# Multiplications by the identity at six places where TensorE waits

## The reference

```python
# first block: mixed attention, then a mixture of 16384 tiny experts (PEER)
s1, s2 = scores of the two query halves against 128 + 128 keys, 8 heads
eidx, gate = the 16 best pairs per head and token, softmax of their scores
act = gelu(x . expert_u[eidx])            # "scores" in the kernel
y   = sum(gate * act * expert_v[eidx])    # "values" in the kernel
# second block
x = x + parallel_mixer(rms_norm(x))                # convolution and a linear recurrence
x = x + cross_attention(rms_norm(x), rms_norm(mem))
x = x + moe(rms_norm(x))                           # 4 groups of 4 experts:
#   best group, its two best experts, out = sum_e combine[e] * (silu(t Wg) * (t Wu)) Wd
out = rms_norm(x)
```

## Time and profile before

| | us |
|---|---|
| Executions shown | 1901.77, 1902.85, 1911.56 |
| Median | 1902.85 |
| Profiled execution, its own time | 1907.88 |
| Its span, first to last instruction | 1906.2 |

### The profile page before, as it was taken

How to read it: one execution, slowest core, us unless ns; L and a number is a source line. 1 busy time by engine, 2 the same in 40 slices (tenths; PEclk the granted TensorE clock), 3 DMA queues, 4 the chain that set the end, 5 groups by cost and what they waited for, 6 DMA issues and landing times.

```text
span 1906.2 us, 25804 instructions
## 1 busy us (share of the span) xinstructions
PE 1840.6 (97%) x10066; PEld 1574.2 (83%) x10066; DVE 1316.9 (69%) x1857; ACT 911.5 (48%) x1013; POOL 77.6 (4%) x101
## 2 busy tenths in 40 slices
PE   8999998999999999999999999989989899999997
PEld 4778766888898888999999999888979778888885
DVE  5788687668998664555555555567865678888887
ACT  2544463412234344444444444455644467667665
POOL 0000000100000341110000000000000000000000
PEclk9999898999999999999999999999999899999999
DMA  7655354434446795666555555554333579898894
GB/s 307 244 190 193 120 206 159 177 111 144 170 150 221 234 284 197 220 203 217 179 195 179 195 178 196 179 199 158 134 140 117 213 304 347 316 354 333 327 351 155
DMA packets 61697, 404.94 MB, mean 212 GB/s; under 512 B 8129, under 2 KB 8417, under 8 KB 15281
## 3 DMA queue, kind: packets, MB, share of 16 engines
q1 hardware_dynamic: 51904, 371.22, 53.2%
q0 software_dynamic: 5968, 20.82, 3.8%
q10 hardware_dynamic: 3746, 11.83, 1.9%
HBM read 391.25 MB, written 12.58 MB: 212 GB/s over the span
## 4 chain that ended last, share of the span: by engine, by line
PE 87%; DVE 6%; DMA 3%; ACT 2%; issue 1%; DVEq 0%; ACTq 0%; SPq 0%
PE ps L2322 23%; PE ps L2323 23%; PE ps L2324 23%; PE ps L2428 7%; PE ps L2725 3%; DMA raw<-in_stream_dram 1%; DMA BIG<-in_stream_dram 1%; PE ps L2901 1%; ACT whi L692 1%; DVE wlo L1239 1%; PE ps L2438 1%; PE ps L2784 1%; PE ps L2559 1%; PE ps L2538 1%; DVE H L1273 0%
## 5 line engine op out<-in xcount | busy, mean ns | idle before, releaser
L1239 DVE TENSOR_TENSOR wlo<-raw,whi 128x2048 fp32r<-128x2048 f32 x179 | 410.1, 2292 | 325.2 <-ACT whi L692 325.1
L692 ACT ACTIVATE whi<-raw 128x2048 fp32r<-128x2048 f32 x179 | 342.9, 1916 | 398.1 <-PE ps L2324 384.6
L2322 PE MATMUL ps<-thi,whi 128*128 128x256 f32 x1056 | 300.7, 285 | 2.1 <-DVE tlo L1256 2.0
L2323 PE MATMUL ps<-tlo,whi 128*128 128x256 f32 x1056 | 300.0, 284 | 0.0
L2324 PE MATMUL ps<-thi,wlo 128*128 128x256 f32 x1056 | 299.9, 284 | 0.0
L2322 PE MATMUL ps<-whi,phi 128*128 128x512 f32 x608 | 239.6, 394 | 7.5 <-DVE plo L1830 6.1
L2322 PE MATMUL ps<-whi,thi 128*128 128x512 f32 (+1 forms) x576 | 228.7, 397 | 10.8 <-DVE wlo L1239 10.7
L2323 PE MATMUL ps<-wlo,phi 128*128 128x512 f32 x608 | 238.5, 392 | 0.0
L2324 PE MATMUL ps<-whi,plo 128*128 128x512 f32 x608 | 237.8, 391 | 0.0
L2324 PE MATMUL ps<-whi,tlo 128*128 128x512 f32 (+1 forms) x576 | 225.1, 391 | 0.0
L2323 PE MATMUL ps<-wlo,thi 128*128 128x512 f32 (+1 forms) x576 | 224.5, 390 | 0.0
(11 more groups left out here) (411 smaller groups left out, 2659.4 us busy)
## 6 DMA issues: line engine op xcount, KB each, us to landing
raw<-in_stream_dram SPq DMA_DIRECT2D x259, 1024.0 KB, 4.8
BIG<-in_stream_dram SPq DMA_DIRECT2D x84, 1024.0 KB, 6.9
BIG<-g_spill POOLq DMA_DIRECT2D x64, 128.0 KB, 4.8
BIG<-in_stream_dram SPq DMA_DIRECT2D x2, 2048.0 KB, 16.4
spare<-in_stream_dram SPq DMA_DIRECT2D x4, 1024.0 KB, 6.1
g_spill<-H ACTq DMA_DIRECT2D x4, 1024.0 KB, 4.8
g_spill<-MOD ACTq DMA_DIRECT2D x4, 1024.0 KB, 4.8
MID<-in_gains_dram POOLq DMA_DIRECT2D x7, 512.0 KB, 4.0
```

Source lines behind the costliest of these rows:

```text
L692: nc.scalar.activation(whi[:, u % 2, :], raw_of(u), ACT.Copy).then_inc(unit_hi, 1)
L1239: nc.vector.tensor_tensor(wlo[:, u % 2, :], raw_of(u), whi[:, u % 2, :].bitcast(f32), ALU.subtract).then_inc(unit_split, 1)
L2322: nc.tensor.matmul(out, ahi, bhi, start=start, stop=False)
L2323: nc.tensor.matmul(out, ahi, blo, start=False, stop=False)
```

## The change

A helper multiplies `ident` by `iota` into 256 columns of a bank that nobody reads at that time, and six calls of it stand ahead of waits. Nobody reads what it writes, and it sets no semaphore.

```diff
+            def run_on(bank, times):
+
+                for _ in range(times):
+                    nc.tensor.matmul(ps[:, bank, 0:S], ident[:, :], iota[:, :], start=True, stop=True)
+
...
+            run_on(2, 9)
             pe.wait_ge(gelu_done, EARLY)
             pe.wait_ge(g_free, 2 * S // GT)
...
+            run_on(7, 8)
             transposes(T_MIX, H)
...
+            run_on(7, 3)
             transposes(T_HX, H)
...
+            run_on(7, 3)
             for k in range(4):
                 t = k // 2
                 pe.wait_ge(rows_ready, ROWS[T_HF] - 2 * TT + k + 1)
...
+            run_on(7, 5)
             pe.wait_ge(grp_ready, 1)
             counts = ps[:, 7, 0:(TT + 1) * N_GRP]
...
+            run_on(6, 3)
             gather(0)
```

## The result

| | executions | median us | range us | ratio to before (95%) |
|---|---|---|---|---|
| Changed kernel, first | 5 | 1891.53 | 1888.16 to 1900.28 | 0.9948 (0.9926 to 0.9970) |
| The same, again | 12 | 1896.09 | 1891.36 to 1906.85 | 0.9974 (0.9957 to 0.9991) |
| The same, a third time | 12 | 1897.48 | 1891.52 to 1903.31 | 0.9971 (0.9958 to 0.9985) |
| Before, beside the last two | 52 | 1902.32 | 1896.79 to 1911.41 | |

The change makes the kernel faster. The first measurement says 11.3 us between the medians (ratio 0.9948), with 1891.53 outside the forecast's range; the 24 later executions of the same kernel have a median of 1896.68, so 5.6 us (0.3%).

The account below looks back on a forecast made before the run. PE's time was taken as the kernel's outside a few waits, at full or half clock. Terms 2.90 + 0 + 2.1 + 2.9 = 7.9 us off 1907.88 give 1900.0; 60% off the median gives 1898.2; between them 1899, range 1893 to 1905.

Parts of the forecast that it names:

- The range: Whole kernel: 1893 (clock held throughout) to 1905 (only the first values gain), about 1 in 10 beyond on either side.
- The gain goes through: First values: full clock from the first product saves 2.90 us, since PE hardly waits from there to 1239 us; bounds 0 and 2.90.
- the prediction's own condition for failure: Fails if the clock falls ahead of the values, or a wait for DVE or a load takes the gain back before 1490.
- The 60%: Whole kernel: from the median only 60% of the 7.9 us gain, 4.7, is taken, giving 1898.2.
- Mixer's norm: Mixer norm's transposes: gain 0, because DVE's low parts fix the first product; bounds -1.7 and +0.2 us.
- the case of the lower bound, -1.7: Mixer's norm: PE idles again behind the transposes and the clock may fall where the products start, half of 3.4 us.
- Cross-attention's norm: Products behind the cross-attention norm: 4.49 us at half clock, of which 2.1 is saved; bounds 0 and 2.1.
- Routing: Router, group counts and gather: 2.9 us saved, between 1.8 (clock fallen in mid-router) and 5.3 (held throughout); bounds -2.9 and 5.3.
- transposes don't hold the clock: Rival, 0.11: at three transpose stages idle time counts on through the transposes; only the values' 2.90 stays, 1905.0.
- Identity times a ramp does not count: Rival, 0.08: added multiplications don't count as work, the clock falls as before, routing runs overrun by 2.9 us: 1910.8 or 1905.8.
- Done already: Rival, 0.13: the profile caught the worst instants; the median execution gains only the first values' part, cut down: about 1902.
- The clock holds through the router as well: Rival, 0.10: routing saves 5.3 us in place of 2.9: 1897.6 from the profile, about 1893 on a good execution.

Follow-up runs that it names:

- with transposes: Changed kernel with each added multiplication replaced by four 128x128 transposes of the identity: 1893.97 us, ratio 0.9951 to the kernel before.
- routing alone: Of the six added runs only the three at the routing (router's transposes, group counts, gather) are kept: 1902.49 us, ratio 0.9998 to the kernel before.
- the last two experiments: Changed kernel with G loads cut to an eighth in the first 18 units, with and without the run of nine: values stage 620.90 and 623.84 us.
- without values: Changed kernel without the run of nine multiplications ahead of the first values, the other five runs standing: 1893.67 us, ratio 0.9956 to the kernel before.
- without the five: Changed kernel without the run of five multiplications ahead of the group counts, the other five runs standing: 1895.54 us, ratio 0.9966 to the kernel before.
- norms alone: Of the six added runs only those ahead of the mixer's and cross-attention norm's transposes are kept: 1899.50 us, ratio 0.9986 to the kernel before.
- values alone: Of the six added runs only the run of nine ahead of the first values is kept: 1902.30 us, ratio 0.9999 to the kernel before.
- twelve-run kernel: Eleven-run kernel plus a run of 3 multiplications ahead of the first attention transposes: 1888.67 us, ratio 0.9925 to the kernel before.
- eleven-run kernel: Changed kernel with five more added runs at idle places followed by half clock: 1887.90 us, ratio 0.9918 to the kernel before.

## Why the prediction was wrong

The direction, the mechanism and most of the places were right; the size was not: 1891.53 first, 1896.7 later, where 1899 was said. Three steps failed, and a loss that the prediction named but counted at nothing, at the mixer's norm, came true in part.

**The range.** "The range goes from 1893 to 1905" was built from the mechanism's cases only. Executions of one kernel spread over 15 us, and the first five had a median 5 us below that of the next 24, of which two are as low as 1891.53 and 21 lie in the forecast's range. A term for where five executions' median falls was missing. Why those five were low isn't settled: three had a clock of 0.990 to 0.993, so less half clock than most; whether by chance or by the chip used, no run tells.

**"The gain goes through"** at the first values. The clock part came as forecast (full clock from 619.17, pace 0.23), and the prediction's own condition for failure, a load that takes it back, came true. In the changed kernel, in order of time:

```profile
703.84 1.92 ACT L692 ACTIVATE whi<-raw 128x2048 fp32r<-128x2048 f32 x1 [4.92 <-DMA raw<-in_stream_dram]
...
708.83 0.47 PE L2322 MATMUL ps<-whi,phi 128*128 128x512 f32 x1 [1.54 <-DVE plo L1830]
```

The 1 MB load for this unit was issued at 695.31 and landed at 703.81, 8.5 us, while a unit's 24 products need 5.4. Before, the load at that point took 6.8 (698.17 to 705.01), and PE didn't wait. PE waited 0.73 to 1.54 us there in seven of the eight profiles with a run ahead of the values and whole loads; the eighth, with transposes, had a load of 6.8 us, no wait, and the shortest stage of them, 621.69. One of the four without a run (routing alone) waited 1.18. The earlier trace rows showed that PE hardly waited, but not how little the loads had to spare; the last two experiments show, in one execution each, that with small G loads the wait is gone and the gain stands. The term was 2.90 and measures 0.7 to 1.1.

**The 60%.** "From the median I therefore take only 60%" rested on the thought that an execution with later falls has part of the gain already. The two sets of executions (24 and 52) say otherwise: the changed kernel is 5.2 us lower at the tenth part of its executions from below (1893.66 against 1898.86), 5.6 at the median, 5.2 at the tenth part from above (1901.07 against 1906.29). Good and bad executions gain alike, since falls vary also where nothing was changed (the column "ahead"). The step's 4.7 us came near the 5.6 only because the sum that it cut, 7.9, was more than 2 too large; and the mean of it with 1900.0, the sum taken off a slow execution, left 3.85.

The other terms, from the stages of the table:
- *Mixer's norm*, forecast 0: 8.16 to 8.21 us with the run, 8.28 to 8.38 without, 0.15. DVE's low parts set the first product, as said. But the case of the lower bound, -1.7 ("the clock may now fall where the products start"), came true in four of eleven profiles with the run, where the fall in the transposes had cost nothing. Three of them are in the table (third, without values, without the five), and their mixer stage took 181.74 to 181.83 us, against 180.35 before and 180.24 with the norms alone. In the first two profiles of the changed kernel it took 181.44 and 181.02 for another reason: the low stretch at 1320 to 1326 lasted 6.8 us in place of 3.4.
- *Cross-attention's norm*, forecast 2.1: 66.56 to 66.59 in four profiles of the table, 68.06 and 68.07 in two where the clock fell 0.4 us after the first product in spite of the run; 68.35 to 68.55 without. 2.0 or 0.4, in the mean 1.4.
- *Routing*, forecast 2.9 between 1.8 and 5.3. Two cases occur: held through the router or most of it, with late counts (router 3.72 to 4.01 us, DVE's wait 1.01 to 1.31, stage 19.93 to 19.95), and fallen in the router (21.55, 21.56). Held throughout, with the counts on time, is in no profile with the runs. Against the mean 23.7 of the three without runs (23.99, 25.46, 21.58) that is 3.8 and 2.1, in the mean of the five profiles 3.1. (One reading in this term is 0.1 off: the second low part would stand at 1518.3, 0.69 behind 1517.61.)

These terms add up to 0.7 + 0.15 + 1.4 + 3.1 = 5.4 us, close to the 5.6 of the 24 executions: the sum without a discount, with the values' term, and a part of the cross-attention's, at their measured size. That it is so close is partly luck. Two columns that no term stands for differ as well and nearly cancel: the mixer took 1.1 us more in the changed kernel's three profiles than before, and the experts 1.5 less, since the low stretch of 3.4 us that stood at 1533.97 before is in none of the three. The profile with the values alone, which has no run at the routing, doesn't have it either, so it isn't shown to be the change's.

Of the rivals, "transposes don't hold the clock" is refuted by the run of transposes alone. The Trainium skill ("TensorE: Matmul & The Clock Gate", Part 4: PE-mode transpose) says that they don't engage the full clock; here 36 of them kept it up for 4.1 us and the products behind them ran at 1.00, so the measurement decides. "Identity times a ramp does not count" fell with the rows at 614.61 and 619.17. "Done already" is out by the medians. "The clock holds through the router as well" is seen for the router at most: in each of those profiles the clock fell late in it or right behind it.

## What to carry to other kernels

A wait of TensorE's can be filled with work that nobody reads. It cost nothing where the filling was shorter than the wait, and it paid where what stood behind ran at half clock and nothing else was late there (the cross-attention's norm, the routing): little where loads became late (the values), and nothing where DVE set the pace and the fall could move onto the products (the mixer's norm). Several places together paid where each alone could hardly be measured. A gain on the bounding engine must be held against how early its loads land, not against how seldom it waited for them. And where executions spread by more than the effect, compare stages between marks of the same engine, and medians of a dozen executions rather than of five.

## What the runs showed of the hardware

Time against the half clock is close to a line: over 35 executions of before the time rises 0.34 us for each us that PE spends at half clock (clock 0.985 at 1896.79 us, 0.977 at 1911.41). In the values' rows about half of each such microsecond was lost in PE's pace (0.427 against 0.2265 us); why it is 0.34 over the whole kernel is not shown, but waits of PE that stand in any case, as at the mixer's transposes, would be one reason. The clock also stayed low while PE was busy: in the run without the five 11.00 of 13.40 us at 0.50, with 20-column and 12-column products among them, and in the twelve-run kernel 6.80 of 6.80 us of small attention products. And it fell without any idle time just ahead: in the eleven-run kernel at 359.3, in the middle of eight multiplications that use 8 rows of the array (356.55 to 361.08); it stayed low for 6.83 us, through the rest of them and most of the 32 records behind (multiplications by the identity), with no gap.
